# When five elementwise products are issued inside the gated delta mixer of a two-block model

## The reference

```
A  = tril(beta * (K K^T) * exp(g_i - g_j), -1)      strictly triangular, c x c
X  = (I + A)^-1
U  = X (beta * V),   W = X (beta * exp(g) * K)
V' = U - W S
O  = (exp(g) * Q) S + tril(Q K^T * exp(g_i - g_j)) V'
S  = exp(g_last) * S + (exp(g_last - g) * K)^T V'
```

## Time and profile before

| | before |
|---|---|
| median of three executions | 3327.61 us (3321.76 to 3332.39) |
| the profiled execution | 3332.39 us |
| its span, first to last instruction | 3330.6 us |
| PE busy | 2794.8 us, 84% |
| DVE busy | 1706.1 us, 51% |
| ACT busy | 1661.1 us, 50% |
| POOL busy | 1144.6 us, 34% |
| mean granted PE clock | 0.897 of full |

### The profile page before, as it was taken

One profiled execution on the slowest core, in us unless ns is written; L12 is line 12 of the kernel. 1 busy time (PEld: TensorE's weight loads), 2 busy tenths in 40 slices (PEclk: granted clock), 3 DMA queues, 4 the chain that ended last, 5 costly groups with the idle time before them and its releaser, 6 DMA issues.

```text
span 3330.6 us, 45056 instructions
## 1 busy us (share of the span) xinstructions
PE 2794.8 (84%) x17472; PEld 2344.1 (70%) x17472; DVE 1706.1 (51%) x3924; ACT 1661.1 (50%) x3325; POOL 1144.6 (34%) x886
## 2 busy tenths in 40 slices
PE   6667776777768777577889999998999999999999
PEld 4465666566656565455568887888999987778887
DVE  6596969696877778345344456554101124521010
ACT  2167676778677867578644223233313222533231
POOL 0023333333233333233133222225645441156463
PEclk8887888788888888578889889999999999999999
DMA  5299999999999999999412000002333321023332
GB/s 190 91 413 358 364 412 409 395 389 416 419 395 381 421 419 420 414 406 387 182 51 70 20 1 1 1 1 70 90 95 86 93 72 43 1 83 95 95 95 76
DMA packets 288967, 701.03 MB, mean 210 GB/s; under 512 B 27824, under 2 KB 207459, under 8 KB 223091
## 3 DMA queue, kind: packets, MB, share of 16 engines
q0 software_dynamic: 73728, 536.90, 39.7%
q1 hardware_dynamic: 215027, 161.26, 15.2%
HBM read 692.34 MB, written 5.77 MB: 210 GB/s over the span
## 4 chain that ended last, share of the span: by engine, by line
PE 52%; DVE 22%; DMA 11%; ACT 9%; issue 4%; POOL 1%; SPq 0%; DVEq 0%; POOLq 0%; ACTq 0%
PE PS L1863 29%; DMA ring<-in_peer_uv,eidx 10%; DVE ring L1549 6%; PE PS L944 4%; ACT ring L1166 2%; PE PS L1011 2%; PE PS L813 1%; DVE acc L2703 1%; PE PS L1762 1%; PE PS L1765 1%; PE PS L1755 1%; DVE W L1362 1%; DMA W<-in_peer_wq 1%; PE PS L1884 1%; PE PS L2081 1%
## 5 line engine op out<-in xcount | busy, mean ns | idle before, releaser
L944 PE MATMUL PS<-C,ring 128*128 128x128 f32 x4096 | 693.4, 321 | 329.7 <-ACT ring L1166 312.7
L944 PEld LDWEIGHTS PS<-C,ring 128*128 128x128 f32 x4096 | 555.9, 165 | 485.9 <-ACT ring L1166 404.1
L728 POOL DMA_INDIRECT ring<-in_peer_uv,eidx x512 | 490.3, 958 | 1125.5 <-DVE act_d L1549 668.6
L1549 DVE CUSTOM_DVE_ANT_0 ring<-ring,PS 128x1024 f32<-128x1024 f32 x512 | 618.4, 1215 | 276.2 <-DMA ring<-in_peer_uv,eidx 269.9
L1166 ACT ACTIVATE ring<-ring,act_d 128x512 f32<-128x512 f32 x1024 | 683.5, 714 | 16.7
L1863 PE MATMUL PS<-held_uH,GW 128*128 128x264 f32 (+1 forms) x3008 | 663.0, 316 | 17.7 <-POOL BIG_value L2420 11.0
L2406 POOL TENSOR_TENSOR GW<-held_wr,GW 128x1024 fp32r<-128x1024 f32 x178 | 429.1, 2412 | 424.2 <-ACT GW L2170 424.2
L1863 PEld LDWEIGHTS PS<-held_uH,GW 128*128 128x128 f32 x3008 | 504.9, 194 | 57.8 <-issue 19.9
L1863 PE MATMUL PS<-BIG_value,GW 128*128 128x264 f32 (+1 forms) x1504 | 448.8, 314 | 0.0
L1863 PE MATMUL PS<-hid,GW 128*128 128x264 f32 (+1 forms) x2304 | 366.5, 321 | 0.0
L1863 PEld LDWEIGHTS PS<-hid,GW 128*128 128x128 f32 x2304 | 332.3, 188 | 33.7
(11 more groups left out here) (502 smaller groups left out, 3793.9 us busy)
## 6 DMA issues: line engine op xcount, KB each, us to landing
held_wr<-in_w_ff SPq DMA_DIRECT2D x128, 512.0 KB, 4.2
wqr<-in_peer_wq SPq DMA_DIRECT2D x32, 512.0 KB
W<-in_peer_wq SPq DMA_DIRECT2D x31, 512.0 KB
held_wr<-in_w_in_ab SPq DMA_DIRECT2D x18, 512.0 KB, 3.8
ring<-in_peer_uv,eidx POOLq DMA_INDIRECT x512
BIG<-in_w_in SPq DMA_DIRECT2D x4, 1536.0 KB, 11.3
held_wr<-in_w_qkv_c SPq DMA_DIRECT2D x12, 512.0 KB, 3.7
w_out<-in_w_out SPq DMA_DIRECT2D x1, 4096.0 KB, 19.0
```

Of the source, the lines that this page charges most:

```text
L728: e.indirect_dma_start(out=rows[:, at:at + 2, :].rearrange("p a d -> p (a d)"), out_offset=None, in_=pairs, in_offset=bass.IndirectOffsetO ...
L944: ins = e.matmul(bank[6 + j // 4][:, j % 4 * P:(j % 4 + 1) * P], row[:, j * P:(j + 1) * P], ident, start=(k == 0 and j % 4 == 0), stop=(k ...
L1549: e.tensor_tensor_reduce(row, row, hn, 1.0, 0.0, ALU.mult, ALU.add, act[:, k:k + 1]).then_inc(*n.up(e_dot))
```

## The change

The three products on POOL are issued before level 1, as soon as kt and vt of that direction are there (two waits are added, on ACT's copies and on DVE's bge), and their own semaphore count moves from behind the level 4 mask to in front of the level 1 mask. PE's wait on the mask is counted accordingly: the product now counts before all masks. qd and gl move on DVE from level 3 to right behind the level 0 update of XT. No instruction is added or taken away, and no operand changes.

```diff
@@ delta_tensor, in the loop over l
-                e.wait_ge(x_pool[d], po + l + (l > 4))
+                e.wait_ge(x_pool[d], po + 1 + l)
@@ delta_pool
             yield
+            e.wait_ge(x_act[d], ac + 2)
+            e.wait_ge(x_dve[d], dv + 2)
+            e.tensor_tensor(w_["vb"][0:c], w_["vt"][0:c], wide(beta), ALU.mult)
+            e.tensor_tensor(w_["kbe"][0:c], w_["kt"][0:c], wide(bge), ALU.mult)
+            e.tensor_tensor(w_["kd"][0:c], w_["kt"][0:c], wide(esf), ALU.mult).then_inc(*up(x_pool[d]))
             yield
...
                 yield
-                if l == 2:
-                    e.tensor_tensor(w_["vb"][0:c], w_["vt"][0:c], wide(beta), ALU.mult)
-                if l == 3:
-                    e.tensor_tensor(w_["kbe"][0:c], w_["kt"][0:c], wide(bge), ALU.mult)
-                if l == 4:
-                    e.tensor_tensor(w_["kd"][0:c], w_["kt"][0:c], wide(esf), ALU.mult).then_inc(*up(x_pool[d]))
                 yield
@@ delta_vector
             e.tensor_tensor(XT, wide(ident2), XT, ALU.subtract).then_inc(*up(x_dve[d]))
+            e.tensor_tensor(qd, conv[:, 0:4, c0:c0 + c], EB, ALU.mult)
+            e.tensor_copy(gl, EB[:, :, c - 1 if d == 0 else 0])
...
-                if l == 3:
-                    e.tensor_tensor(qd, conv[:, 0:4, c0:c0 + c], EB, ALU.mult)
-                    e.tensor_copy(gl, EB[:, :, c - 1 if d == 0 else 0])
```

## The result

The changed kernel takes 3348.77 us (median of five, 3341.67 to 3358.59). Against the kernel before the ratio is 1.0065 (95% interval 1.0048 to 1.0082), some 21 us more, where +10.4 was forecast. Its profiled execution took 3351.76 us, with a span of 3349.8.

A forecast was written before the change was run, and what follows sets the result against it. PE, busy for 93% of the mixer, was taken to set the pace. The terms 6.1 - 2.3 + 5.6 + 1 = +10.4 us, on the median of 3327.61, gave 3338 us; range 3324 to 3349.

The forecast's parts named there:

- What bounds the mixer: Mixer: PE, busy 338.62 of 365 us (93%), sets the pace; an edit counts by its effect on PE's pauses.
- The early part, +6.1: L1747 of direction 1: early POOL products hold DVE's two-input operations, lengthening PE's wait; +6.1 us, bounds 0 to 7.5.
- Level 4, -2.3: L1762 at level 4: qd and gl no longer delay L2575, so PE waits less; -2.3 us, at most 5.9.
- Level 0, +5.6: DVE at level 0: qd and masks delay L2575, lengthening PE's L1762 wait at level 2; +5.6 us, bounds 0 to 13.
- The copy gl: DVE's gl: taken as not held by POOL; if held, up to 1.0 us ten times, perhaps 4 us more, 3342 us.
- PE's clock, +1 (at most 3.6): Mixer: longer pauses may bring more stretches at 1.2 GHz; between 0 and 3.6 us, taken as +1.
- slower by far: Pauses in steps 0 and 1 lower PE's clock for longer, or L2500 and L2501 are held: +15 to +28 us; chance 0.12.
- The first (early part free): DVE and POOL hardly hinder each other in the early part; only the DVE part remains, +3.3 us, 3331; chance 0.16.
- the hidden case: Mixer: all costs are hidden and only the gain at level 4 counts, -2.3 us, 3325; chance 0.08.
- The faster case: Levels 2 to 4: L2587 no longer held by products, adding to the 2.3; -10.3 us, 3317; chance 0.04.
- Its sign: Changed kernel's profile: a mean mixer clock under 0.93 would mean the clock is the larger term.

The follow-up runs named there:

- qd_level2: The kernel before with only qd and gl moved on DVE from level 3 to level 2: ratio 1.0012 (1.0000 to 1.0025).
- dve_only: Against the kernel before, only qd and gl move behind level 0's XT; the POOL products stay on levels 2 to 4: ratio 1.0046, +15 us.
- after_fill: The changed kernel plus eight small unread matmuls in PE's pause ahead of L1747 of direction 1: 3340.28 us, ratio 1.0034 to the kernel before.
- memset_early: The changed kernel with its three POOL products replaced by memsets of the same tiles: 3340 us, ratio 1.0035 to the kernel before.
- pause_fill: The kernel before plus two spare DVE products ahead of direction 1's L2510 and eight unread matmuls in PE's wait there: ratio 1.0014, +5 us.
- before_fill: The kernel before plus five small unread matmuls in PE's pause ahead of L1747 of direction 1: ratio 0.9996, -1 us.
- pause_only: The kernel before plus two spare DVE products ahead of direction 1's L2510, nothing moved: ratio 1.0062, +21 us.

## Why the prediction was too low

- **What bounds the mixer: right.** PE sets the pace; everything found is a wait or a slowdown of PE.
- **The early part, +6.1: right.** L1747 and L1819 wait 4.9 + 1.6 = 6.5 us more. I had booked all of it at L1747, but a quarter stands at L1819, because PE waits for the held L2585 itself. L2585 was held to the end of a product, L2499 and L2500 (0.30 to 0.32 us beside products) were not. With memsets in the products' place the wait is 7.6 us again.
- **Level 4, -2.3: right in size.** The five waits at L1762 of level 4 go from 7.4 to 5.1 us. Whether they are worth that much time is another matter: qd_level2 removes the same, and no gain can be told in its time.
- **Level 0, +5.6: not there in the changed kernel.** At level 2 L1762 waits longer in one step only, by 1.15 us (first row below against 1.42); in the others as before. In step 3 the slow clock itself took the room: from the transpose to the end of level 1 PE was 3 us slower, and DVE, late by qd, was in time for it (read from the timeline, not tested by itself). Where the clock is up at that place the wait is there: L1762 waits 13.5 + 1.8 us in dve_only and 13.5 + 2.0 in after_fill, against 10.2 in qd_level2, which is 5.1 and 5.3 us for level 0. So the size was right and the sum was not: a fall behind L1747 and a longer wait at level 2 did not both come in one step of the changed kernel. The one wait that did grow brought a fall of its own:

```profile
2054.52 1.77 PE L1762 MATMUL PS<-GW_value 106*106 106x106 f32 x8 [2.57 <-ACT GW_value L2129]
```

- **The copy gl: wrong.** I took it as never held, by L2577's row. Direction 1's copy in step 3 took 0.98 us beside a mask of 1.01, where that of direction 0, 1.7 us earlier, took 0.16:

```profile
2129.47 1.01 POOL L2388 TENSOR_TENSOR GW_value<-GW_value,held_C 106x424 f32<-106x424 f32 x1 [3.19 <-PE PS L1755]
...
2129.52 0.98 DVE L2523 COPY delta<-held_uH_value 128x4 f32<-128x4 f32 x1
```

  The Trainium skill, SBUF — State Buffer, section Who interferes with whom, says that an SBUF copy can contend with GpSimd. The trace agrees, with 0.98 us; I had argued against it with the row of another copy. In this step PE's next wait at L1762 is 1.22 us, as before.
- **PE's clock, +1 (at most 3.6): the step that failed.** It measured 12: PE's busy time grew by 12.0 us for the same matmuls. With the waits (+5.3) that makes the 17.3 of the mixer. I took a quarter of the slow time as the bound for no reason that a row gave, and wrote that no row of L1747's waits showed the clock falling for long. The rows were there. In the kernel before, the waits at L1747 are 2.13, 1.75, 1.05, 1.05 and 1.47 us in steps 0 to 4, and the granted clock of the steps is 0.89, 0.90, 1.00, 1.00 and 1.00. In step 1 the matmuls behind the 1.75 are slow:

```profile
1958.06 0.58 PE L1747 MATMUL PS<-held_C,delta 106*106 106x106 f32 x4 [1.75 <-DVE delta L2510]
...
1960.66 1.77 PE L1755 MATMUL PS<-GW_value 106*106 106x106 f32 x8
...
1962.22 1.65 PE L1755 MATMUL PS<-delta 106*106 106x106 f32 x8
```

  My own sum put all five waits over 2 us. Priced with these rows, three more steps with a fall at about 3.1 us each give +9 instead of +1, and the sum +13 without the level 0 term, +18 with it. Two of the three falls came behind L1747 (steps 3 and 4, waits of 1.65 and 2.04 us), the third behind the wait of 2.57 at level 2 of step 2. The mean of the mixer, 0.96, hid that two steps had falls and three had none. Not every fall is one of L1747: at the border of steps 0 and 1 of the kernel before, the granted clock is 0.50 from 1936.4 to 1949.8 us, behind a wait of 1.28 at L1827 for ACT, and the changed kernel has the same. The rule of the mixer's clock stood in my last rival (*slower by far*, 0.12), against which I held just the row that I had not looked up.

- **The rivals.** The first (early part free) and the hidden case fall with the waits at L1747. The faster case falls too: L2585 is held less at the later levels (0.30 and 0.38 us in step 3, though 1.08 once in step 2 beside a mask), and L1762's wait falls at level 4 only, by the 2.3 us that qd left. The last, slower by far, is what happened, by its clock half; its other half, L2500 and L2501 held, did not. Its sign, a granted clock of the mixer under 0.93, was met to the rounding: the row says 0.93, before 0.96. The total of about 21 us is that of this rival and not of the forecast.

**What stays open.** The length of the wait alone does not decide. In step 2 of the changed kernel the clock stayed up behind 1.64 us at L1747 and fell at the wait of 2.57; in step 3 it fell behind 1.65. The wait of 1.47 us at L1747 in step 4 brought a fall in memset_early and in qd_level2 (first row; there too the eight records take 1.72), and none in the kernel before (second row):

```profile
2189.71 1.72 PE L1755 MATMUL PS<-GW_value 104*104 104x104 f32 x8
...
2191.72 0.98 PE L1755 MATMUL PS<-GW_value 104*104 104x104 f32 x8
```

A wait of 1.42 us brought one in pause_fill. Behind the waits of 1.04 to 1.06 at L1747 none was seen. So a single profiled execution tells where falls were, not how many the usual execution has, and the 12.0 us above is the figure of one pair of executions.

Nor is it shown why before_fill and qd_level2, whose mixers were 6 and 5 us shorter in their profiles, are no faster in time. A likely reason lies in the profile that they are compared with: that execution of the kernel before took 3332.39 us, 4.8 over its median, and for 12 of the 13 other kernels the timed difference to it is higher than that of the two mixers (by 5 us in the median). Its own mixer would then have been some us longer than usual. No second profile of it was taken to show this. The 2 us outside the mixer are within what two executions differ by (2954 to 2964 us over all fourteen profiles).

## What to carry to other kernels

A wait of the busiest engine is not worth its length only. Before pricing an edit that lengthens PE's waits by half a microsecond, look, wait by wait, how long the same matmuls take behind the short ones and behind the long ones, and price each wait that grows into the second kind with that difference (here 0.6 us of wait brought 3 us of slow matmuls). That price is an upper one, since waits of equal length brought a fall in one kernel and none in another. A granted clock averaged over several steps can't show this; cut it by step. To tell wait from clock on the chip, put in the wait alone, and then the wait with matmuls in it whose results nobody reads.

## What the runs showed of the hardware

- The clock of PE falls although PE is busy for 92% of the mixer: behind single waits of 1.65 to 2.06 us (step 3 of the changed kernel, of pause_only), with some 3.1 us lost in the first of them, and in some kernels behind 1.42 to 1.48. Matmuls whose result nobody reads mostly keep it up (pause_only against pause_fill, 16 us).
- The granted clock in the records and the durations of equal matmuls agree in place: 0.50 from 2126.1 to 2132.7 us of the changed kernel, where eight records take 1.65 to 1.77 instead of 0.91 to 0.99.
- A DVE tensor_scalar of 128 x 128 is held by POOL memsets too, for as long as they last: 0.53 and 0.48 us instead of 0.29 (memset_early, step 1), each ending 0.08 us after a memset ended.
- A DVE copy of 128 x 4 from SBUF to SBUF takes 0.16 us alone and 0.98 to 1.01 beside a POOL mask, which reads two SBUF operands (changed kernel, dve_only); copies of 128 x 1 were never over 0.147.
